# The Hyena transform split by even and odd times, with part of the first modulation and some spectrum rows on VectorE

## The chip, the core and the metric

The kernel runs on one core of one Trainium2 chip. The metric is the device time of one execution in microseconds (us), as the median of repeated runs. PE is the matmul engine (TensorE), PEld its weight loads, DVE VectorE, ACT ScalarE, POOL GpSimd and SP SyncE.

## The reference

One inference step of a two-layer backbone over 128 context tokens and 512 latent tokens with D_MODEL = 1024. Each layer modulates its input, projects it, runs windowed attention and a Hyena branch side by side, merges the two by gates, and then runs a feed-forward part. What the change touches is the modulation and the long convolution of the Hyena branch:

```python
mod = jax.nn.silu(cond) @ lp['w_ada'] + lp['b_ada']        # w_ada (1024, 6144); sh1, sc1 are its first 2048 columns
h = x * (1.0 + sc1) + sh1

def bidir_long_conv(u, h, bias):                            # u (1, L, 512), L = 512 latent or 128 context
    g = jnp.concatenate([h[:, 0], jnp.zeros((1, C)), h[:0:-1, 1]], axis=0)
    U = jnp.fft.rfft(u, n=2 * L, axis=1)
    G = jnp.fft.rfft(g, n=2 * L, axis=0)
    y = jnp.fft.irfft(U * G[None], n=2 * L, axis=1)[:, :L]
    return y + u * bias
```

h is the output of a small sine MLP times a decaying window; it depends on the weights alone, so its spectrum G can be made ahead of the layer.

## The kernel before

All of it is written by hand for each engine, in program order, with semaphores between the engines; nothing is scheduled. Every large matmul is done as three fp32r products of a value split into a high part and a low part (hi x hi, hi x lo, lo x hi). ACT makes the high part by a copy, DVE makes the low part by a subtraction. `split(g)` does this for a streamed weight chunk of up to 2048 columns (`raw` to `whi`, `wlo`; two slots), and SP loads the next chunk into `raw` once the low part of the chunk before has been made. `STREAM` is the order of the chunks and `GEMM` the order of the work.

**The opening** (once, until the first projection of q). PE makes the sine MLP, then the filter rows of both layers (`filter_rows`, 10 blocks a layer), the transforms of these (`g_spectrum`, five pairs a layer, `GSP_PAIRS` is their order), and the first two parts of the modulation, sh1 and sc1, as eight chunks `ada(0)` to `ada(7)` of four fp32 matmuls each with two output rows, whose results are transposed to columns (`col_mm`). DVE multiplies the filter rows with their windows, adds and subtracts them (`filter_blocks`) and makes low parts. ACT makes high parts and copies the spectra out of PSUM (`g_rows`), POOL writes them to DRAM (`g_spill`). The later modulation parts are not made on PE but on DVE, as products with whole rows of the transposed w_ada (`ada_t`, four instructions a chunk), and lie between the gates and the feed-forward tiles of layer 0. After `modulation`, ACT makes the modulated rows (`h_make`), POOL their low parts, and PE begins `opening(0, ...)`, the q projection.

**The Hyena stage** (once in each layer). A transform of length 2L over real input is taken as matmuls with cosine and sine matrices. Before this stage the input xu lies channel by token; PE transposes it by 128 tokens (`u_transposed`), DVE folds the four latent blocks into two sums and two differences (`ufold`), and PE transforms (`spectrum`): pair 0 is the context, pairs 1 and 2 the even frequencies of the latent tokens out of two folded blocks each, pairs 3 and 4 the odd ones out of all four blocks. A pair is a real and an imaginary PSUM row of 128 frequencies x 512 channels. DVE multiplies a pair with the stored spectrum (`prod`, `us`, six operations), ACT and DVE split the product into `yhi` and `ylo`, and PE transforms it back (`inverse`) onto all 512 times in `ax`. The matrices come in four chunks F0, I0, F1 and I1. Between them PE does the projection of the attention output (`attn_projected`, 24 matmuls each). Then comes gate 0, whose eight steps each wait for one low row made on DVE (`h_lo_row`, semaphore `hg_ready`), and DVE also joins the result, the bias and x0 for the next matmul (`hy_src`).

## Time and profile before

| | |
|---|---|
| median of 3 runs | 2062.82 us (2062.6 to 2062.84) |
| the profiled execution's own time | 2061.39 us |
| its span, first to last instruction | 2059.6 us |
| mean granted TensorE clock | 0.992 of full speed |
| PE busy | 2016.4 us, 98% of the span |
| DVE busy | 1142.6 us, 55% |
| ACT busy | 747.6 us, 36% |
| POOL busy | 184.0 us, 9% |
| PE's share of the chain that ended last | 90% |

PE's matmuls overlap each other in the pipeline: one of them is listed with a duration longer than the distance to the next one's start. So what a matmul costs is read as the distance between starts. The busy shares are averages over stages; how far another engine is from being the limit has to be read stage by stage.

### The profile page before, as it was taken

How to read it: one execution, taken by the hardware profiler on the slowest of the kernel's cores; microseconds unless marked ns; L12 is line 12 of the kernel's file. 1: busy time of each engine (PE TensorE's matmuls, PEld its weight loads, DVE VectorE, ACT ScalarE, POOL GpSimd, SP SyncE). 2: the span in 40 equal slices, each digit the busy share in tenths (PEclk: the TensorE clock that was granted, in tenths of full speed). 3: DMA queues.
4: the chain of work that ended last, by engine and by line, in shares of the span. 5: the costliest groups of instructions: out<-in, count | busy, mean ns of one | idle time of the engine just before them, and what ended most of it. 6: DMA issues, size and time to landing. Idle time of an engine off the chain costs nothing.

```text
span 2059.6 us, 30339 instructions
## 1 busy us (share of the span) xinstructions
PE 2016.4 (98%) x13030; PEld 1917.8 (93%) x13030; DVE 1142.6 (55%) x1682; ACT 747.6 (36%) x1103; POOL 184.0 (9%) x202
## 2 busy tenths in 40 slices
PE   8999999999999999999999999999999999999997
PEld 3589998999989999999998999899998999999996
DVE  6416457777556767776545454863246433233435
ACT  3354453522264321333244443452226332133323
POOL 0120001200141000000031000120015000000011
PEclk9999999999999999999999998999999999999998
DMA  8331112254313335434322101222221212212121
GB/s 313 143 124 64 39 62 92 88 179 165 125 59 123 138 133 197 178 126 154 105 71 82 65 21 60 98 77 82 82 83 47 90 63 71 90 65 79 63 71 52
DMA packets 37726, 207.07 MB, mean 101 GB/s; under 512 B 4326, under 2 KB 7959, under 8 KB 18904
## 3 DMA queue, kind: packets, MB, share of 16 engines
q1 hardware_dynamic: 31192, 185.04, 25.1%
q0 software_dynamic: 3312, 13.35, 1.8%
q10 hardware_dynamic: 3088, 6.75, 0.9%
q8 instruction: 102, 1.67, 0.3%
q14 instruction: 32, 0.26, 0.0%
HBM read 196.98 MB, written 8.14 MB: 100 GB/s over the span
## 4 chain that ended last, share of the span: by engine, by line
PE 90%; DVE 4%; ACT 3%; issue 1%; DMA 1%; SPq 0%; POOL 0%; ACTq 0%; DVEq 0%
PE gemm_psum L609 50%; PE gemm_psum L639 15%; PE gemm_psum L662 3%; PE gemm_psum L682 3%; PE gemm_psum L622 3%; PE aux_psum L749 3%; PE aux_psum L802 2%; PE gemm_psum L788 2%; PE aux_psum L730 2%; PE gemm_psum L551 2%; PE gemm_psum L515 1%; PE aux_psum L738 1%; ACT h_src_rows L1174 1%; PE aux_psum L772 1%; DMA ada_early<-in_ada 1%
## 5 line engine op out<-in xcount | busy, mean ns | idle before, releaser
L609 PE MATMUL gemm_psum<-h_hi,w_hi 128*128 128x322 f32 x2144 | 497.2, 313 | 0.3
L609 PE MATMUL gemm_psum<-h_hi,w_lo 128*128 128x322 f32 x2144 | 493.5, 311 | 0.0
L609 PE MATMUL gemm_psum<-h_lo,w_hi 128*128 128x322 f32 x2144 | 492.1, 311 | 0.0
L609 PEld LDWEIGHTS gemm_psum<-h_hi,w_hi 128*128 128x128 f32 x2144 | 362.5, 189 | 4.4 <-issue 3.1
L609 PEld LDWEIGHTS gemm_psum<-h_lo,w_hi 128*128 128x128 f32 x2144 | 362.7, 189 | 0.0
L609 PEld LDWEIGHTS gemm_psum<-h_hi,w_lo 128*128 128x128 f32 x2144 | 362.2, 189 | 0.0
L1574 DVE TENSOR_TENSOR w_lo<-w_raw,w_hi 128x2048 fp32r<-128x2048 f32 (+3 forms) x130 | 251.3, 1933 | 198.7 <-ACT w_hi L1104 197.7
L1104 ACT ACTIVATE w_hi<-w_raw 128x2048 fp32r<-128x2048 f32 (+3 forms) x130 | 209.6, 1612 | 170.1 <-PE gemm_psum L639 65.6
L1562 DVE CUSTOM_DVE_ANT_0 aux_psum<-w_raw,cond_by_row 128x1024 f32<-128x1024 f32 x160 | 190.9, 1256 | 6.9 <-DMA w_raw<-in_ada_t 6.4
L1707 DVE SCALAR_TENSOR_TENSOR x<-gemm_psum,mod,x 128x128 f32<-128x128 f32 (+2 forms) x144 | 55.4, 434 | 157.8 <-PE gemm_psum L639 128.0
L639 PE MATMUL gemm_psum<-act_hi,w_lo 128*128 128x322 f32 x616 | 141.9, 311 | 0.0
L639 PE MATMUL gemm_psum<-act_lo,w_hi 128*128 128x322 f32 x616 | 141.6, 311 | 0.0
L639 PE MATMUL gemm_psum<-act_hi,w_hi 128*128 128x322 f32 x616 | 141.5, 311 | 0.0
L1609 DVE SCALAR_TENSOR_TENSOR gate_acc<-gate_rows,par,gate_acc 128x642 f32<-128x642 f32 x88 | 80.2, 911 | 75.7 <-ACT gate_acc L1182 74.0
L1780 DVE TENSOR_TENSOR gate_acc<-gate_acc,gemm_psum 128x644 f32<-128x644 f32 x40 | 33.0, 826 | 144.1 <-PE gemm_psum L609 144.1
L639 PEld LDWEIGHTS gemm_psum<-act_hi,w_hi 128*128 128x128 f32 x616 | 104.3, 189 | 0.0
L639 PEld LDWEIGHTS gemm_psum<-act_hi,w_lo 128*128 128x128 f32 x616 | 104.2, 189 | 0.0
L639 PEld LDWEIGHTS gemm_psum<-act_lo,w_hi 128*128 128x128 f32 x616 | 103.9, 189 | 0.0
L1123 ACT ACTIVATE act_hi<-gate_acc 128x644 fp32r<-128x644 f32 x44 | 32.7, 742 | 154.0 <-DVE gate_acc L1780 147.6
L1181 ACT ACTIVATE gate_rows<-gemm_psum 128x644 f32<-128x644 f32 (+1 forms) x48 | 31.8, 663 | 144.8 <-PE gemm_psum L609 140.4
L662 PE MATMUL gemm_psum<-h_hi,w_hi 128*128 128x322 f32 x224 | 72.8, 325 | 11.6 <-POOL h_lo L2052 3.7
L1583 DVE TENSOR_TENSOR w_lo<-w_raw,w_hi 128x1024 fp32r<-128x1024 f32 x32 | 38.0, 1221 | 80.2 <-ACT w_hi L1119 80.2
(337 smaller groups left out, 3276.0 us busy)
## 6 DMA issues: line engine op xcount, KB each, us to landing
w_raw<-in_w_up SPq DMA_DIRECT2D x44, 1024.0 KB, 4.8
w_raw<-in_ada_t SPq DMA_DIRECT2D x40, 1024.0 KB, 4.7
w_raw<-in_w_down SPq DMA_DIRECT2D x32, 704.0 KB, 4.2
w_raw<-in_w_gate SPq DMA_DIRECT2D x16, 1024.0 KB, 4.7
w_raw<-in_w_z SPq DMA_DIRECT2D x12, 1024.0 KB, 4.7
w_raw<-in_w_out SPq DMA_DIRECT2D x8, 1024.0 KB, 4.7
g_kept<-g_rows_out POOLq DMA_DIRECT2D x10, 512.0 KB, 2.9
ada_early<-in_ada SPq DMA_DIRECT2D x4, 1024.0 KB, 20.4
```

The lines of the kernel that those rows point to most:

```text
L551: last = mm(gp[:, 2 + r % 2, :], w[s][:, cols_], v[:, pl, :], start=kb == 0 and n == 0, stop=kb == len(places) - 1 and n == 2)
L609: last = mm(gp[:, 2 * (t % 2) + hf, 0:HALF], w[:, off + P * kk:off + P * (kk + 1)], moving(kk, lo)[:, hf * HALF:(hf + 1) * HALF], start=kk ...
L622: last = mm(gp[:, 2 * (t % 2) + hf, 0:HALF], w[:, off + P * kk:off + P * (kk + 1)], moving(kk, lo)[:, half(hf)], start=kk == 0 and n == 0, ...
L639: last = mm(gp[:, 2 * (t % 2) + hf, 0:HALF], w[:, off + P * kk:off + P * (kk + 1)], moving(kk, lo)[:, half(hf)], start=kk == 0 and n == 0, ...
L662: last = mm(banks(c, p_, hf), w[:, P * (KD * c + kk):P * (KD * c + kk + 1)], (hlo if lo else hhi)[:, kk, half(hf)], start=kk == 0 and n == ...
L682: last = mm(gp[:, 2 * ((t0 + c) % 2) + hf, 0:HALF], w[:, P * (KD * c + kk):P * (KD * c + kk + 1)], moving(kk, lo)[:, hf * HALF:(hf + 1) * ...
L749: last = mm(ax[:, 2, HD * n:HD * (n + 1)], p_t(n)[:, P * kb:P * (kb + 1)], v[:, HD * (n % 2):HD * (n % 2 + 1)], start=kb == 0, stop=kb == ...
L1104: run(whi[s][:, 0:n], raw[st_ % 2][:, 0:n], ACT.Copy).then_inc(sem["w_hi"], raised("w_hi"))
L1562: V.tensor_tensor_reduce(out=ax[:, 2 * gr:2 * gr + 2, :].rearrange("p a b -> p (a b)"), in0=raw[n % 2][:, D_MODEL * (t % 2):D_MODEL * (t % ...
L1574: TT(wlo[s][:, 0:n], raw[STEP[(lane.layer, "g", g)] % 2][:, 0:n], f32(whi[s][:, 0:n]), ALU.subtract).then_inc(sem["w_split"], raised("w_sp ...
L1609: STT(acc[:, 1:ROW - 1], z[:, a:a + ROW - 2], w(tap), acc[:, 1:ROW - 1], ALU.mult, ALU.add).then_inc(sem[event if tap else "dve_order"], r ...
L1707: STT(x[:, m, a:b], gp[:, 2 * (t % 2) + h, a - HALF * h:b - HALF * h], mod[:, gate + m, gr:gr + 1], x[:, m, a:b], ALU.mult, ALU.add)\
```

## The change

The transform of the latent tokens is taken apart once more. The latent times are put in the order even, odd (`u_cols` takes every second token in the transposes, and the constants, filter features and windows are permuted alike). Pairs 3 and 4 now each transform only two blocks (one the even times, one the odd), and sums and differences of the two give the odd frequencies; that sum is a new step on ACT and DVE for the input (`odd_out`, `ureg`) and on POOL for the stored spectra (`g_combine`). Back-transforms write 256 of the 512 columns each, and DVE puts the halves together at the end, with two operations on each half. Four chunks of matrices become three (F0, F1, I0), and the order of the work around them is rewritten. Apart from that, the last two of the eight early modulation chunks go from PE to DVE (`ada_t(0, 6)`, `ada_t(0, 7)`, between the filter blocks of layer 1, with an own SBUF buffer `ada_out` for the products), and the last six spectrum rows of the opening are copied out by DVE (`g_rows_late`) and not by ACT.

```diff
-F0_BLOCKS, F1_BLOCKS = 14, 16
+F0_BLOCKS, F1_BLOCKS = 12, 10
-        + [("F", 0), ("pa", 0), ("I", 0), ("F", 1), ("I", 1)]
+        + [("F", 0), ("pa", 0), ("F", 1), ("I", 0)]
-    G_V = [(0, 1), (2, 3), (4, 5), (6, 7, 8, 9), (6, 7, 8, 9)]
+    G_V = [(0, 1), (2, 3), (4, 5), (6, 8), (7, 9)]
...
         g_spectrum(0, 4)
-        filter_rows(1, 4, 6)
+        filter_rows(1, 4, 8)
         ada(4)
+        filter_rows(1, 8, 10)
         g_spectrum(0, 1)
-        filter_rows(1, 6, 8)
+        g_spectrum(0, 2)
         ada(5)
-        g_spectrum(0, 2)
-        filter_rows(1, 8, 10)
-        ada(6)
-        ada(7)
         g_spectrum(1, 0)
...
-                    at = 512 * (2 * ((pair_ - 1) % 2) + o)
+                    at = 256 * (2 * (pair_ - 1) + o)
                     for n, (y, w) in enumerate(((yhi, whi), (yhi, wlo), (ylo, whi))):
-                        last = mm(ax[:, j, :], y[:, ys, o, P * j:P * (j + 1)], w[slot][:, at:at + 512],
+                        last = mm(out(j), y[:, ys, o, P * j:P * (j + 1)], parts(w[slot][:, at:at + 256]),
...
+            for n in (2, 3):
+                pe.wait_ge(sem["pa_out"], due("pa_out", n - 1))
+                attn_projected(n)
+            pe.wait_ge(sem["w_split"], due("w_split", gF1 + 1))
...
+            spectrum(3, U_V[3])
+            spectrum(4, U_V[4])
             pe.wait_ge(sem["w_split"], due("w_split", gI + 1))
...
+            for pair_ in range(1, PAIRS):
+                inverse(pair_, slot_of(gI), pair_ == 1, pair_ == PAIRS - 1)
...
+                if l and m == 1:
+                    dve.wait_ge(sem["cond_rows"], 1)
+                    ada_t(0, 6)
...
+                if l and n == 0:
+                    ada_t(0, 7)
+                if l and n == 1:
+                    first_modulation()
...
+        def g_rows_late(r0, r1):
+            for r in range(r0, r1):
+                dve.wait_ge(sem["gsp_mm"], 10 + r + 1)
+                V.tensor_copy(gst[:, GSP_PAIRS[r // 2], r % 2, :], gp[:, 2 + r % 2, :]).then_inc(sem["gsp_late"], 1)
...
+            for o in range(2):
+                first = ureg[:, 2 * o, :]
+                TT(ureg[:, 2 * o + 1, :], first, spec_bank(8 + o), ALU.subtract).then_inc(sem["usp_out"], raised("usp_out"))
+                dve.wait_ge(sem["usp_out"], now("usp_out"))
+                TT(first, first, spec_bank(8 + o), ALU.add).then_inc(sem["usp_out"], raised("usp_out"))
...
-                STT(xu[:, j, LAT], xu[:, j, LAT], parc("hy_bias", j), ax[:, j, :], ALU.mult, ALU.add)\
+                for a in range(2):
+                    STT(rows[:, a], rows[:, a], parc("hy_bias", j), same, ALU.mult, ALU.add)\
+                dve.wait_ge(sem["dve_order"], now("dve_order"))
+                for a, op in ((0, ALU.add), (1, ALU.subtract)):
+                    TT(rows[:, a], rows[:, a], turned, op).then_inc(sem["dve_order"], raised("dve_order"))
...
+        def g_combine(l):
+            for o in range(2):
+                G.tensor_tensor(g_first[:, o, :], gst[:, 3, o, :], gst[:, 4, o, :], ALU.add).then_inc(sem["g_halves"], 1)
+            pool.wait_ge(sem["g_halves"], 4 * l + 2)
+            for o in range(2):
+                G.tensor_tensor(gst[:, 4, o, :], gst[:, 3, o, :], gst[:, 4, o, :], ALU.subtract).then_inc(sem["g_halves"], 1)
```

Three places show how the rows of an engine move. The first is DVE in the opening, at the filter blocks of layer 1 (m = 1, then m = 2). Before, the next window products (`filter_prod`) follow at once:

```order
L1511 TENSOR_TENSOR filter_sums<-filter_prod 128x512
L1513 TENSOR_TENSOR d_block<-filter_prod 128x512
L1501 TENSOR_TENSOR filter_prod<-aux_psum,windows 128x512 x2
L1489 TENSOR_TENSOR filter_lo<-d_block,filter_hi 128x512
L1511 TENSOR_TENSOR filter_sums<-filter_prod 128x512
```

After the change four row products stand between them (`ISA mod` is the read of the accumulated sum):

```order
L1571 TENSOR_TENSOR d_block<-filter_prod 128x512
L1525 ISA ada_products,mod<-w_raw,cond_by_row 128x1024
L1525 ISA mod 128x1
L1525 ISA ada_products,mod<-w_raw,cond_by_row 128x1024
L1525 ISA mod 128x1
L1525 ISA ada_products,mod<-w_raw,cond_by_row 128x1024
L1525 ISA mod 128x1
L1525 ISA ada_products,mod<-w_raw,cond_by_row 128x1024
L1525 ISA mod 128x1
L1559 TENSOR_TENSOR filter_prod<-aux_psum,windows 128x512 x2
```

So the window products of m = 2 stand behind one chunk of the modulation, and the same happens once more before `first_modulation`.

The second place is DVE in the Hyena stage, between the products of pair 2 and the first low row of the odd pairs. Before, one odd pair took these rows, and the last of them are the low parts that PE waits for:

```order
L1842 TENSOR_TENSOR prod<-gemm_psum,g_spec 128x512
L1845 TENSOR_TENSOR u_spec<-gemm_psum,g_spec 128x512
L1847 TENSOR_TENSOR u_spec<-gemm_psum,g_spec 128x512
L1848 TENSOR_TENSOR prod<-gemm_psum,g_spec 128x512
L1852 TENSOR_TENSOR u_spec<-u_spec 128x512
L1857 TENSOR_TENSOR u_spec<-prod 128x512
L1587 TENSOR_TENSOR y_lo<-u_spec,y_hi 128x512 x2
```

After the change both odd pairs go through together: four sums and differences (L1920, L1922), a first block of six, and then a second block of six, four sums and the low parts as here:

```order
L1932 TENSOR_TENSOR prod<-u_blocks,g_spec 128x512 x2
L1932 TENSOR_TENSOR u_spec<-u_blocks,g_spec 128x512 x2
L1934 TENSOR_TENSOR u_blocks<-prod 128x512
L1935 TENSOR_TENSOR u_blocks<-u_spec 128x512
L1939 TENSOR_TENSOR u_spec<-u_blocks 128x512
L1939 TENSOR_TENSOR prod<-u_blocks 128x512
L1939 TENSOR_TENSOR u_spec<-u_blocks 128x512
L1939 TENSOR_TENSOR prod<-u_blocks 128x512
L1631 TENSOR_TENSOR y_lo<-u_spec,y_hi 128x512
L1631 TENSOR_TENSOR y_lo<-prod,y_hi 128x512
```

The first low row of pair 3 now stands behind 20 operations, and not behind six.

The third place is DVE behind the back-transform, where the result is joined. Before, a channel block took one operation between two low rows of gate 0:

```order
L1881 SCALAR_TENSOR_TENSOR xu<-xu,par,aux_psum 128x512 x2
L1587 TENSOR_TENSOR h_lo<-h_src_rows,h_hi 128x644
L1881 SCALAR_TENSOR_TENSOR xu<-xu,par,aux_psum 128x512
L1587 TENSOR_TENSOR h_lo<-h_src_rows,h_hi 128x644
L1881 SCALAR_TENSOR_TENSOR xu<-xu,par,aux_psum 128x512
L1587 TENSOR_TENSOR h_lo<-h_src_rows,h_hi 128x644
```

After the change it takes four of half the size:

```order
L1955 SCALAR_TENSOR_TENSOR xu<-xu,par,aux_psum 128x2x128 x2
L1959 TENSOR_TENSOR xu<-xu,aux_psum 128x2x128 x2
L1631 TENSOR_TENSOR h_lo<-h_src_rows,h_hi 128x644
L1955 SCALAR_TENSOR_TENSOR xu<-xu,par,aux_psum 128x2x128 x2
L1959 TENSOR_TENSOR xu<-xu,aux_psum 128x2x128 x2
```

Each low row of gate 0 thus stands behind four joining operations where it stood behind one.

## Rows read from the trace of the kernel before

**Rows 1.** The page's head and its busy times by engine.
```profile
span 2059.6 us, 30339 instructions
PE 2016.4 (98%) x13030; PEld 1917.8 (93%) x13030; DVE 1142.6 (55%) x1682; ACT 747.6 (36%) x1103; POOL 184.0 (9%) x202
```

**Rows 2.** The waits of PE over the whole run: us in total, times, longest.
```profile
PE gemm_psum L551 <- ACT g_rows_out L1056: 2.8, 2, 1.7
```

**Rows 3.** Timeline of PE in layer 0's Hyena stage: start us, us, instruction.
```profile
337.99 0.46 PE L772 MATMUL gemm_psum<-attn_lo,w_hi 128*128 128x322 f32 x2
...
338.28 0.46 PE L772 MATMUL gemm_psum<-attn_hi,w_lo 128*128 128x322 f32 x2
...
339.28 0.40 PE L802 MATMUL aux_psum<-w_hi,y_hi 128*128 128x512 f32 x1
...
339.51 0.39 PE L802 MATMUL aux_psum<-w_lo,y_hi 128*128 128x512 f32 x1
...
372.22 0.47 PE L682 MATMUL gemm_psum<-h_hi,w_hi 128*128 128x322 f32 x2
...
386.75 0.54 PE L609 MATMUL gemm_psum<-hy_hi,w_hi 128*128 128x322 f32 x2
```

**Rows 4.** Busy x count of PE, PEld, DVE, ACT, POOL from 372 to 387 us.
```profile
372.00:387.00 15.00, 14.93 (x100) 14.65 (x99) 14.64 (x18) 14.75 (x24) 10.93 (x7) 1.00 0.12 45
```

**Rows 5.** Timeline of PE in the opening; in brackets idle before and releaser.
```profile
61.35 3.60 PE L515 MATMUL gemm_psum<-w_raw,cs 128*2 128x512 f32 x8
...
111.58 0.39 PE L662 MATMUL gemm_psum<-h_hi,w_hi 128*128 128x322 f32 x1 [2.15 <-ACT g_rows_out L1056]
```

**Rows 6.** Timeline of DVE in the opening.
```profile
57.47 0.68 DVE L1513 TENSOR_TENSOR d_block<-filter_prod 128x512 f32<-128x512 f32 x1
...
90.19 0.17 DVE L1547 SCALAR_TENSOR_TENSOR mod<-gemm_psum,par 128x16 f32<-128x16 f32 x1
```

**Rows 7.** The page's group of products with a row of w_ada (busy, mean ns).
```profile
L1562 DVE CUSTOM_DVE_ANT_0 aux_psum<-w_raw,cond_by_row 128x1024 f32<-128x1024 f32 x160 | 190.9, 1256 | 6.9 <-DMA w_raw<-in_ada_t 6.4
```

**Rows 8.** Timeline of POOL, then of DVE, around 320 us.
```profile
319.81 5.67 POOL L2104 TENSOR_TENSOR v_lo<-u_blocks,v_hi 128x512 fp32r<-128x512 f32 x4
...
322.55 1.76 DVE L1852 TENSOR_TENSOR u_spec<-u_spec 128x512 f32<-128x512 f32 x1
```

**Rows 9.** Timeline of DVE in layer 0's Hyena stage.
```profile
319.97 0.68 DVE L1842 TENSOR_TENSOR prod<-aux_psum,g_spec 128x512 f32<-128x512 f32 x1
...
328.24 0.68 DVE L1842 TENSOR_TENSOR prod<-gemm_psum,g_spec 128x512 f32<-128x512 f32 x1
...
335.32 2.28 DVE L1574 TENSOR_TENSOR w_lo<-w_raw,w_hi 128x2048 fp32r<-128x2048 f32 x1
...
337.52 1.12 DVE L1868 SCALAR_TENSOR_TENSOR xu<-xu,par,aux_psum 128x128 f32<-128x128 f32 x4
...
343.54 0.68 DVE L1842 TENSOR_TENSOR prod<-gemm_psum,g_spec 128x512 f32<-128x512 f32 x1
...
348.90 0.68 DVE L1842 TENSOR_TENSOR prod<-gemm_psum,g_spec 128x512 f32<-128x512 f32 x1
...
373.34 1.39 DVE L1881 SCALAR_TENSOR_TENSOR xu<-xu,par,aux_psum 128x512 f32<-128x512 f32 x2
...
382.39 0.82 DVE L1587 TENSOR_TENSOR h_lo<-h_src_rows,h_hi 128x644 fp32r<-128x644 f32 x1
```

**Rows 10.** Granted clock in the opening, third from the end of the row.
```profile
113.00:114.00 1.00, 1.00 (x6) 1.00 (x5) 1.00 (x2) 0.97 (x3) 0.00 (x0) 0.50 1.01 410
```

**Rows 11.** Timeline of PE over the same attention tail in layers 0 and 1.
```profile
295.11 0.43 PE L749 MATMUL aux_psum<-par,p_t 128*128 128x64 f32 x2 [0.18 <-ACT p_t L1140]
...
305.96 0.55 PE L609 MATMUL gemm_psum<-h_hi,w_hi 128*128 128x322 f32 x2
...
1259.90 0.43 PE L749 MATMUL aux_psum<-par,p_t 128*128 128x64 f32 x2 [0.17 <-ACT p_t L1140]
...
1277.29 0.55 PE L609 MATMUL gemm_psum<-h_hi,w_hi 128*128 128x322 f32 x2
```

More of the change, by code:

```diff
@@ L72, in stream @@
 def stream():
-    order = [(0, "pre", 0), (0, "pre", 1)] + [(0, "ada", s) for s in range(ADA_EARLY, ADA_FIRST)]
+    order = [(0, "pre", 0), (0, "pre", 1)] + [(0, "ada", s) for s in (6, 4, 7, 5)]
     for layer in range(DEPTH):
@@ L1835, in _ @@
             split(gA)
[L1836 removed]
+            for p_ in range(3):
                 gr, gi = gsp[:, G_SLOT[p_], 0, :], gsp[:, G_SLOT[p_], 1, :]
@@ L2189, in _dft_constants @@
     k4 = np.arange(P)
+    two = [2 * np.arange(P) + b for b in range(2)]
     lat = []
@@ L2192, in _dft_constants @@
         re, im = forward(4 * k4 + add, DEC_SEQ // 2, N)
+        br, bi = back(4 * k4 + add, DEC_SEQ // 2, N)
         if add == 0:
```

291 lines of the change are left out of this document (174 added, 117 removed).

## The prediction, made before the changed kernel ran

> **What bounds the kernel now.** I began with the page's busy times: PE is busy for 2016.4 of 2059.6 us, DVE for little more than half [rows 1]. Then the list of PE's waits: it waits almost nowhere; one of the longest entries is 2.8 us in two pieces, for copies of spectrum rows in the opening [rows 2]. So work taken off PE shortens the kernel until another engine's chain reaches it. Then PE's timeline where the change acts. The distance of two starts is 0.233 us for 512 columns (339.28 to 339.51) and 0.148 us for 322 (337.99 to 338.28, two matmuls in between) [rows 3]. The busy times by stage show what the page's average hides: around gate 0 of layer 0, from 372 to 387 us, DVE is busy 14.64 of 15 us and ACT 14.75 [rows 4]. There PE has company already, and this decides the forecast.
>
> **What leaves PE.** Odd pairs: 12 matmuls of 512 less for each of two pairs, so 24 x 0.233 = 5.6 us in each `spectrum` stage, and 2 x 5.6 = 11.2 us in the opening for both layers' `g_spectrum`. Back-transforms: 96 matmuls a layer fall from 512 to 256 columns. No row shows 256; the price lies between half of the 512 (0.117) and the 322's 0.148. I take 0.119, since the 512 and the 322 lie nearly on a line through zero, and it is nearest to the half: 96 x 0.114 = 11.0 us a layer, at least 8.2. `ada(6)` and `ada(7)`: the eight passes of one chunk are one row of 3.60 us from 61.35 on [rows 5], of which some 0.1 lies over what follows; two chunks are 7.0 us. Four transposes of two columns less are 0.3. The sum off PE is 18.5 us in the opening and 16.6 in each layer, 51.7 in all.
>
> **The opening: DVE and ACT become the pace.** Layer 1's filter block m = 1 ends now at 57.47 + 0.68 = 58.1 us [rows 6], having waited for PE before; with the halved spectra I put its end at 56. Then `ada_t(0, 6)`: 4 x 1.256 = 5.0 us [rows 7]. At the same time POOL runs `g_combine(0)`, four additions of 128x512. The row on POOL's pace for that size is 5.67 us for four, and during it a DVE operation with both inputs in SBUF took 1.76 us, where the same line later took 0.69 [rows 8]: 1.07 us is what one of them pays. With three of the four products meeting POOL I add 3.2 us (bounds: 0 and, with six operations met, 6.4). DVE is at 64.3. PE has come to filter row 8 at about 60.5 and waits 4 us. From there DVE runs nearly without a pause to the modulation: three blocks of five operations at 0.60 (319.97 and the rows behind it, [rows 9]) are 9.3 with waits, two and two operations around `ada_t(0, 7)` 2.7, that chunk 5.0, the sums 0.8: the modulation is done at 82.1 against 90.3 now [rows 6], 8.2 earlier.
> From the modulation to the first projection matmul there are 21.3 us now (90.3 to 111.58, [rows 5]); in this stretch PE loses 24 matmuls (5.6 us), while ACT gets three high parts more and loses six copies to DVE. I take 5.6 as the gain and no more, because each spectrum row still waits for a copy of the one two before. That would be 13.8; for ACT's three high parts more I take 13.5 us for the whole opening. Bounds: 18.5, PE's full relief, and 8, if the meeting with POOL costs 6.4 and the copies on DVE queue behind the splits. The weight split and ACT's Silu on the row of conditions (one copy-sized 2048 operation) lie in ACT's idle time before its next high part, and cost nothing; without that cover they would cost 2 us. The transfer of that row, 1 MB, now goes out in the crowded start; nobody needs it before 56 us, so I cost it at nothing.
>
> **The Hyena stage: DVE again.** Its first product starts at 319.97 and the last low row of gate 0 at 382.39 for 0.8 [rows 9]. After the change DVE has these pieces, each from a row of its present timeline:
> pair 0, 8.3 (319.97 to 328.24, unchanged); the split of F1, 1280 columns, 1.4 (2048 take 2.2: 335.32 to 337.52); pair 1 6.4 (7.1 less a wait for ACT's split); pair 2 5.4 (343.54 to 348.90); the split of I0 2.2; the context's join 1.1; four sums and differences 2.8; twelve operations of two products 7.8; four sums 2.5; four low parts 2.8; the split of gate 0's weights 2.2; the context times x0 0.7; low rows 0 to 2 with ACT's pace 4.1. That reaches 367.7. From low row 2 to the end of low row 7 it is 10.9 us now; the joins add to it: a 512 operation takes 0.66 to 0.70 and a 128 one 0.28 (1.12 for four), so 256 columns are about 0.41 by the line between them, and a channel block costs 4 x 0.41 against 0.66, with one wait between: +0.9 each, +3.7 for four. Low row 7 ends at 319.97 + 61.5 = 381.5.
> PE in the same time: it does four `attn_projected` and the context back-transform before it needs an odd spectrum, reaches back-transform 3 at about 350 and finds its input not made: 8.7 us idle, until the first low part at 358.7. Back-transforms 3 and 4 end at 364.4, gate 0 then follows the low rows, and after the last one 18 matmuls remain (2.7 us): 384.2 against 386.6, where gate 0 ends now (386.75 is the next row, [rows 3]). So of 16.6 us taken off PE in a layer, 2.4 reach the end, and the rest becomes two idle stretches. Bounds: 6, if the joins cost half and no operation meets POOL, and a loss of 1, if a strided operation of 256 costs as much as one of 512. After gate 0 nothing waits longer: DVE is done 1.6 us sooner than now.
> The Trainium skill (GPSIMD Engine Reference, Specifications) says that GpSimd's SBUF interfaces are shared with VectorE and are contended by VectorE instructions with two SBUF inputs. The trace agrees in 1.76 against 0.69 us. By that rule the new products from `ureg` and the row products, both with two SBUF inputs, are exposed and the joins out of PSUM are not; it makes the time of `g_combine` worth as much as its count.
>
> **The sum.** 2061.4 (the profiled execution's own time) - 13.5 - 2 x 2.4 = 2043.1. The median of the runs stands 1.4 above the profiled one, so 2044.5.
>
> **The rivals.**
> *PE stays the only bound.* If the DVE pieces overlap better than I lay them, the 51.7 us come in full: 2011. Against it stands DVE's 14.64 of 15 us before anything is added. A half-way form, with the opening at its bound and 6 a layer, gives 2061.4 - 18.5 - 12 + 1.4 = 2032. Chance 0.12 for both.
> *The clock gives it back.* In the opening PE started again at 111.58 after a gap, and at 113 us its granted clock was 0.50, the lower level of 1.2 GHz [rows 10]. The same attention tail took 10.9 us in layer 0 (295.11 to 305.96) and 17.4 in layer 1 (1259.90 to 1277.29), where the clock was at the lower level for most of it [rows 11]: 6.5 us for one spell. Now there will be a gap of 8.7 us in each layer. If the clock is low only for back-transforms 3 and 4, they take up to 5 us more, of which 3.3 are hidden, since DVE asks for them at 367.7 only. If it stays low through gate 0 as well, its 96 matmuls at 0.268 (0.148 x 1.8) take 25.7 us and end at 395: 8.7 us later than now in each layer, in all 2061.4 + 17.4 - 13.5 + 1.4 = 2067, slower than before. It decides from about 5 us of loss a layer on. Against it: gate 0 keeps PE nearly nine tenths busy even at DVE's pace. Chance 0.05.
> The Trainium skill (TensorE: Matmul & The Clock Gate, Part 1) has it that the array idles at 1.2 GHz and sustained activity releases 2.4 GHz. By that alone the restart behind the gap is slow and then recovers within the back-transforms; the sum would be the same as mine, and only a stage with short gaps would fall to the rival.
> *The spells move.* The spell of 6.5 us in layer 1 has no cause in the program that layer 0 lacks. With another timing it may vanish (2038) or strike both layers (2051). I leave the likeliest at one and put both into the range.
> *Nothing gained.* If the meeting with POOL and the copies behind splits cost their worst (opening +8 only) and the joins cost full size, 2061.4 - 8 + 2 + 1.4 = 2057, with a second spell 2063. Chance 0.09.
>
> **How the numbers follow.** The forecast with the moving spells holds 0.74; it spans 2036 to 2054. The range for 8 in 10 takes in the half-way form and the worst bound: 2033 to 2057. About 0.2%, 4 us, is what a measurement of this kernel can tell from no change. Below 2058.7 lie the forecast, the first rival and a third of the last: 0.89; the rest of the last is within 0.2%: 0.06; above 2066.9 lies the clock's rival: 0.05.
>
> **What would show it.** PE busy about 50 us less; PE idle before back-transform 3 for 7 to 10 us in each layer, released by DVE's `y_lo`; idle steps in gate 0 released by `h_lo` on DVE; 256-column matmuls 0.12 us apart; a PE wait of 3 to 5 us for `filter_prod` near 60 us with POOL's additions beside `ada_products`; the first projection at 98 us and gate 0's end 16 us earlier than now. I am wrong if `y_lo` of pair 3 comes within 3 us of PE, if the 256-column joins measure 0.3 or 0.6, or if the clock is at 0.50 through gate 0.

## The result and the profile after

| | before | after |
|---|---|---|
| median | 2062.71 us (2061.13 to 2062.84, 4 runs) | 2029.58 us (2029.05 to 2031.81, 4 runs) |
| ratio | | 0.9843, 95% interval 0.9826 to 0.986 |
| first projection starts | 111.58 [rows 5] | 97.39 |
| PE busy | 2016.4 [rows 1] | 1963.9 |

The kernel is 33.1 us faster; 18.3 were forecast (2061.4 less 2043.1). A second occasion, told below, gave the changed kernel nearly the same time (2030.42) and the kernel before a median of 2055.89. One execution of a variant (`copies_act`), the one that was profiled, took 3191 us at a mean granted clock of 0.556; its time is left out, and of its trace only durations on DVE and POOL are used.

The page's head and its busy times by engine, after:

```profile
span 2026.9 us, 30168 instructions
...
PE 1963.9 (97%) x12914; PEld 1881.4 (93%) x12914; DVE 1168.8 (58%) x1743; ACT 740.6 (37%) x1098; POOL 195.6 (10%) x210
```

The waits of PE over the whole run (total, times, longest), after:

```profile
PE aux_psum L819 <- DVE y_lo L1631: 16.1, 2, 8.1
...
PE aux_psum L545 <- DVE filter_prod L1559: 4.6, 1, 4.6
...
PE gemm_psum L691 <- DVE h_lo L1631: 2.4, 6, 0.8
```

The timeline of PE, after, with the idle time before and its releaser in brackets:

```profile
64.57 2.93 PE L545 MATMUL aux_psum<-w,h2T 128*128 128x512 f32 x3 [4.57 <-DVE filter_prod L1559]
...
97.39 0.39 PE L671 MATMUL gemm_psum<-h_hi,w_hi 128*128 128x322 f32 x1 [0.89 <-DVE w_lo L1627]
...
297.16 0.62 PE L797 MATMUL aux_psum<-v_first,w_hi 128*128 128x512 f32 x2
...
328.29 0.28 PE L819 MATMUL aux_psum<-w_hi,y_hi 128*128 128x256 f32 x1
...
328.41 0.28 PE L819 MATMUL aux_psum<-w_lo,y_hi 128*128 128x256 f32 x1
...
342.13 0.58 PE L819 MATMUL aux_psum<-w_hi,y_hi 128*128 128x256 f32 x1 [8.03 <-DVE y_lo L1631]
...
366.58 0.46 PE L618 MATMUL gemm_psum<-hy_hi,w_hi 128*128 128x322 f32 x2
...
1256.91 0.62 PE L797 MATMUL aux_psum<-v_first,w_hi 128*128 128x512 f32 x2
...
1326.35 0.46 PE L618 MATMUL gemm_psum<-hy_hi,w_hi 128*128 128x322 f32 x2
```

PE has 116 matmuls less (48 in the two `g_spectrum`, 48 in the two `spectrum` stages, 16 of `ada`, 4 transposes) and is busy 52.5 us less, against the 51.7 of the working; both busy times hold some work at the low clock. The wait for `y_lo` is new, 8.0 us in each layer before back-transform 3 (342.13), and so is the one for `filter_prod` (64.57). 256 columns are 0.12 us apart (328.29 to 328.41).

The timeline of DVE, after:

```profile
55.94 2.29 DVE L1525 CUSTOM_DVE_ANT_0 ada_products<-w_raw,cond_by_row 128x1024 f32<-128x1024 f32 x1
...
63.83 1.28 DVE L1559 TENSOR_TENSOR filter_prod<-aux_psum,windows 128x512 f32<-128x512 f32 x2
...
82.22 0.17 DVE L1547 SCALAR_TENSOR_TENSOR mod<-mod,par 128x8 f32<-128x8 f32 x1
...
303.93 0.68 DVE L1887 TENSOR_TENSOR prod<-aux_psum,g_spec 128x512 f32<-128x512 f32 x1
...
349.98 0.83 DVE L1631 TENSOR_TENSOR h_lo<-h_src_rows,h_hi 128x644 fp32r<-128x644 f32 x1 [0.88 <-ACT h_hi L1356]
...
350.73 0.87 DVE L1955 SCALAR_TENSOR_TENSOR xu<-xu,par,aux_psum 128x256 f32<-128x256 f32 x2
...
351.63 0.75 DVE L1959 TENSOR_TENSOR xu<-xu,aux_psum 128x256 f32<-128x256 f32 x2
...
362.92 0.81 DVE L1631 TENSOR_TENSOR h_lo<-h_src_rows,h_hi 128x644 fp32r<-128x644 f32 x1
```

The modulation is done at 82.4 us (82.22 and the row's 0.17), the first product of the Hyena stage starts at 303.93 and the last low row of gate 0 ends at 363.7.

Windows of the changed kernel; the third number from the end is the granted clock. The first two and the last are its low stretches, the third is layer 1's attention tail:

```profile
62.00:69.00 7.00, 4.43 (x7) 2.23 (x8) 6.93 (x13) 0.63 (x1) 0.96 (x2) 0.51 0.85 303
...
338.00:346.00 8.00, 3.87 (x20) 3.87 (x21) 7.97 (x11) 4.19 (x7) 0.17 (x3) 0.57 0.00 0
...
1242.00:1256.00 14.00, 14.00 (x114) 14.00 (x113) 8.09 (x13) 6.00 (x11) 0.54 (x1) 1.00 0.32 115
...
1297.00:1308.00 11.00, 6.14 (x29) 6.14 (x30) 10.28 (x15) 6.43 (x11) 0.83 (x4) 0.53 0.10 23
```

And the same tail in the kernel before, [rows 11]:

```profile
1263.00:1277.00 14.00, 14.00 (x71) 14.00 (x71) 3.84 (x7) 3.20 (x6) 0.54 (x1) 0.51 0.30 109
```

**Where the time came from.** The matmuls between two marks are the same in both kernels outside the opening and the stage, so the span can be cut at marks on PE. The marks of before that [rows 3, 5] don't show are the first transform of each layer and the end of layer 1's gate 0:

```profile
313.19 0.63 PE L788 MATMUL aux_psum<-v_first,w_hi 128*128 128x512 f32 x2
...
1284.52 0.62 PE L788 MATMUL aux_psum<-v_first,w_hi 128*128 128x512 f32 x2
...
1358.07 0.54 PE L609 MATMUL gemm_psum<-hy_hi,w_hi 128*128 128x322 f32 x2
```

| stretch | before | after | gained | forecast |
|---|---|---|---|---|
| start to first projection | 111.58 | 97.39 | 14.2 | 13.5 |
| to layer 0's first transform | 201.61 | 199.77 | 1.8 | 0 |
| layer 0's first transform to the end of gate 0 | 73.56 | 69.42 | 4.1 | 2.4 |
| to layer 1's first transform | 897.77 | 890.33 | 7.4 | 0 |
| layer 1's stage, the same marks | 73.55 | 69.44 | 4.1 | 2.4 |
| to the end of the span | 701.53 | 700.55 | 1.0 | 0 |
| sum | 2059.6 | 2026.9 | 32.7 | 18.3 |

Two stretches where the change touches nothing gave 9.2 us. Both held a stretch of low clock before ([rows 10, 11]) and hold none now. They are not alike. The 7.4 us are a low stretch that is gone. The 1.8 us belong to one that can also fall earlier: in three other profiles of the kernel before (experiment 2) PE's clock is low at about 88 to 95 us (in one of them behind the first projection as well), the first projection starts at 113.1 to 113.4 and the first transform at 313.4, 313.4 and 314.7, no sooner than the 313.19 here. In the second profile of the changed kernel the clock is low from 84 to 92 us, and the first projection starts at 99.05. So the opening is uncertain by about 1.7 us in either kernel, and the first two rows are better read together: 16.0 us from these two profiles, 14.6 from the others (313.4 less 298.79), 13.5 forecast. The last stretch, 1.0 us, is within what it varies by itself (700.4 to 702.2 us in the changed kernel and its variants).

### The profile page after: what moved, and what is told of

It reads as the page before. It is cut to its first block, busy times and chain, and to the rows that moved or that the text cites. A ratio compares the mean times of both kernels' runs of the same rounds, so it can differ in the third digit from the quotient of the medians.

```text
span 2026.9 us, 30168 instructions
## 1 busy us (share of the span) xinstructions
PE 1963.9 (97%) x12914; PEld 1881.4 (93%) x12914; DVE 1168.8 (58%) x1743; ACT 740.6 (37%) x1098; POOL 195.6 (10%) x210
## 4 chain that ended last, share of the span: by engine, by line
PE 83%; DVE 10%; ACT 4%; issue 2%; ACTq 0%; DMA 0%; POOL 0%; SPq 0%; DVEq 0%
PE gemm_psum L618 51%; PE gemm_psum L648 15%; PE gemm_psum L671 3%; PE gemm_psum L631 3%; PE aux_psum L758 2%; PE gemm_psum L691 2%; PE aux_psum L739 2%; PE aux_psum L747 1%; ACT h_src_rows L1186 1%; PE gemm_psum L525 1%; DVE aux_psum L1793 1%; PE gemm_psum L563 1%; DVE w_lo L1618 1%; DVE x L1797 1%; PE aux_psum L545 1%
## 5 line engine op out<-in xcount | busy, mean ns | idle before, releaser
L1618 DVE TENSOR_TENSOR w_lo<-w_raw,w_hi 128x2048 fp32r<-128x2048 f32 (+4 forms) x128 | 244.6, 1911 | 182.1 <-ACT w_hi L1116 181.1
L1116 ACT ACTIVATE w_hi<-w_raw 128x2048 fp32r<-128x2048 f32 (+4 forms) x128 | 204.1, 1594 | 170.7 <-PE gemm_psum L648 65.6
L1135 ACT ACTIVATE act_hi<-gate_acc 128x644 fp32r<-128x644 f32 x44 | 32.7, 742 | 153.5 <-DVE gate_acc L1824 147.1
L2159 POOL TENSOR_TENSOR sums<-x 128x644 f32<-128x644 f32 x4 | 6.4, 1589 | 790.5 <-DVE x L1751 790.5
```

The source lines that it names most:

```text
L1116: run(whi[s][:, 0:n], raw[st_ % 2][:, 0:n], ACT.Copy).then_inc(sem["w_hi"], raised("w_hi"))
L1618: TT(wlo[s][:, 0:n], raw[STEP[(lane.layer, "g", g)] % 2][:, 0:n], f32(whi[s][:, 0:n]), ALU.subtract).then_inc(sem["w_split"], raised("w_sp ...
```

## The experiments

Times are medians; where a run is one execution it says so. The kernel before was measured beside each set, but since its own time turns out to fall into two groups, variants are compared with the changed kernel's 2029.6 and 2030.4, and by marks in their traces.

**1. The changed kernel again.** No edit.

> The changed kernel as it is, measured beside the kernel before on another occasion. Theory (part of the 33 us was a stretch of lower clock that the kernel before happened to have in its four executions): where the kernel before takes 2053.7 and not 2062.7, the changed kernel still takes 2029 to 2031, and the gain is 23 to 25 us, ratio 0.988. Rival (the change itself removed the stretch): the gain is 33 us, ratio 0.984.

2030.42 us (2030.23 to 2030.69, 4 runs); before 2055.89 (2053.21 to 2062.57, 9 runs); ratio 0.9871, interval 0.9851 to 0.9891. The first theory holds: the changed kernel's time stayed, and the gain fell to 25.5 us. Over all sets the kernel before ran 37 times: 16 executions at 2052.9 to 2056.8 us, 21 at 2059.6 to 2063.2, none between. Where the clock was listed the first group had a mean of 0.995 to 0.997, the second 0.991 to 0.994. Four of the sets, each on another chip, hold executions of both groups, so it is not the chip that decides. The changed kernel's eight executions lie between 2029.0 and 2031.8 (median 2030.3). Against the medians of the groups, 2053.9 and 2061.5, the gain is 24 us over the first and 31 over the second; the first occasion, with four executions of the second group, gave 33.

**2. Shifting layer 1.** The same matmul repeated in layer 0's feed-forward, 14, 28 or 56 times in the kernel before, 28 times in the changed one:

```diff
+            if lane.layer == 0 and GEMM[g] == ("down", 3):
+                for _ in range(14):
+                    mm(gp[:, 2 * (t % 2), 0:HALF], whi[s][:, off:off + P], moving(0, False)[:, half(0)], start=True, stop=True)
```

> The kernel before with 14 repeated 322-column matmuls (2.1 us) in layer 0's feed-forward, in front of a down projection; the same product is written again. It shifts all of layer 1. Theory (timing): whether the clock falls in layer 1's attention tail depends on when the tail comes, not on what the program does there: with some of the shifts of 2.1, 4.1 and 8.3 us the low stretch is shorter, longer or gone, and the time differs from 2062.7 plus the shift by up to 6.6 us. Rival (the program's own activity): the low stretch stays at the same place of the program and as long in all three, and this kernel takes 2064.8.

> The same with 28 matmuls, 4.1 us. Theory (timing): the low stretch in layer 1's attention tail (13.6 us from 1263) moves against the program, and the time is not 2062.7 + 4.1 = 2066.8. Rival (the program's own activity): 2066.8, with the stretch moved along by 4.1.

> The same with 56 matmuls, 8.3 us. Theory (timing): the low stretch in layer 1's attention tail moves against the program or is gone; gone it would be 2062.7 + 8.3 - 6.6 = 2064.4. Rival (the program's own activity): 2071.0.

> The changed kernel with the same 28 matmuls in layer 0's feed-forward, 4.1 us. Theory (timing): layer 1's attention tail, which had the full clock, may fall to the lower one: 2029.6 + 4.1 = 2033.7, or up to 6.6 more, 2040. Rival (the change itself took away what made the clock fall): the tail keeps the full clock, 2033.7.

One execution each: 2055.8, 2059.2, 2064.15 and, changed, 2034.51. The tail of the kernel before with 14 more matmuls; then the end of gate 0, the longer of the two waits of PE in the tail, and layer 1's first transform:

```profile
1263.00:1277.00 14.00, 12.81 (x107) 12.81 (x108) 8.85 (x16) 6.32 (x12) 0.54 (x1) 1.00 0.43 151
```

```profile
387.00 0.54 PE L609 MATMUL gemm_psum<-hy_hi,w_hi 128*128 128x322 f32 x2
...
1264.19 0.43 PE L752 MATMUL aux_psum<-par,p_t 128*128 128x64 f32 x2 [1.23 <-DVE p_t L1676]
...
1279.85 0.62 PE L791 MATMUL aux_psum<-v_first,w_hi 128*128 128x512 f32 x2
```

The tail has the full clock in all four. From 387.00 to 1279.85 it is 892.85 us; less the 2.1 put in, 890.8, against 897.77 before: the low stretch costs 7.0 us (by the kernels with 28 and 56 matmuls 7.0 and 6.8). That the stretch belongs to the program's own activity is refuted. That the shift removed it is not shown: the kernel before, unshifted, took 2055.62 on that occasion, in the first group too. Nor do PE's waits in the tail settle it. The kernel before waits there for 0.17 us [rows 11] and, with its clock about to fall, for 1.22:

```profile
1262.34 0.44 PE L749 MATMUL aux_psum<-par,p_t 128*128 128x64 f32 x2 [1.22 <-DVE p_t L1673]
```

The three shifted kernels wait for 0.16 to 0.18 and 1.22 to 1.23 us at the same places and keep the full clock.

**3. The two parts moved to DVE, taken back singly.** `ada_back` has `ada(6)` and `ada(7)` on PE, `rows_back` has all spectrum rows on ACT:

```diff
-ADA_ROWS = 6
+ADA_ROWS = 8
...
+        ada(6)
+        ada(7)
         g_spectrum(1, 0)
```

```diff
-    LATE_ROWS = 14
+    LATE_ROWS = 20
...
-                    if d in (1, 2):
+                    if d:
                         g_rows(1, 1 + d, 2 + d)
...
-                g_rows_late(4, 8)
```

> The changed kernel with the last two early modulation chunks back on PE (7.0 us of PE more, 10 us of DVE less); all else stays. Theory (trade): in the changed kernel PE waited 4.6 us near 60 us for DVE and then ran some 2.7 us slower at the lower clock, so the 7.0 us were given back on the spot: the wait near 60 us vanishes, the first projection stays within 1 us of 97.4 us, and the time within 2 us of the changed kernel's 2029.6. Rival (relief, as the prediction had it): the 7.0 us off PE came through to a good part: the first projection is 3 to 6 us later, at 100 to 103 us, the time about 2034.

> The changed kernel with the last six spectrum rows of the opening copied by ACT again, between its own pieces of the modulated rows. Theory (ACT's pace): a pair of ACT's modulated row and copy takes 1.9 us, a spectrum row on PE 1.4, so six rows take some 3 us more: the first projection at 100 to 101 us, the time 3 us above the changed kernel's 2029.6. Rival: DVE's copies also stand in front of the low part of the first weights, which released the first projection, so that taking them off it gives the time back: the first projection within 0.7 us of 97.4.

2033.16 (4 runs) and 2035.7 us (4 runs). PE in `ada_back`: its window matmuls start at 60.02 without a wait, but the first projection at 101.40.

```profile
60.02 1.98 PE L545 MATMUL aux_psum<-w,h2T 128*128 128x512 f32 x4
...
101.40 0.39 PE L673 MATMUL gemm_psum<-h_hi,w_hi 128*128 128x322 f32 x1 [1.04 <-DVE w_lo L1622]
```

The first projection of the changed kernel was at 97.39 in one profile and at 99.05 in that of the second occasion.

So the move of the two chunks gained 2.4 to 4.0 us there and 2.7 to 3.6 in the time: nearer to the relief than to the trade that I put first. In `rows_back` an ACT copy is what the first projection waits for:

```profile
101.10 0.61 PE L671 MATMUL gemm_psum<-h_hi,w_hi 128*128 128x322 f32 x1 [0.89 <-ACT g_rows_out L1068]
```

The first projection comes 2.1 to 3.7 us later, near the 3 expected, and the time is 5.3 to 6.1 us more. In the profiled execution, which took 2037.81 us and was the slowest of the four, another 2.5 us lie in the restart behind the first projection: it is 202.25 us to the first transform against 199.77, with the clock at 0.52 from 100 to 107 us. Whether the other three have it is not known.

**4. POOL's additions left out.** `g_combine` for layer 0 is not done, so its odd spectra stay unsplit sums.

```diff
+            if l:
                 for o in range(2):
                     G.tensor_tensor(g_first[:, o, :], gst[:, 3, o, :], gst[:, 4, o, :], ALU.add)...
```

> The changed kernel without POOL's four additions of g_combine for layer 0 (left out: layer 0's odd spectra stay the sums over even and over odd times). Theory (the additions on POOL cost DVE about 1 us for each two-input operation beside them): the row products of the first modulation chunk take 1.22 us each and not 2.2, the window products come 4 us sooner and PE's wait near 60 us is under 1 us. Rival (the products are slow there for another reason, the transfers of the opening): they take 2.2 us all the same.

One execution, 2026.88. DVE's row product, then PE's window matmuls and the first projection:

```profile
56.52 1.22 DVE L1525 CUSTOM_DVE_ANT_0 ada_products<-w_raw,cond_by_row 128x1024 f32<-128x1024 f32 x1
...
60.95 1.98 PE L545 MATMUL aux_psum<-w,h2T 128*128 128x512 f32 x4 [0.55 <-DVE filter_prod L1559]
...
94.90 0.39 PE L671 MATMUL gemm_psum<-h_hi,w_hi 128*128 128x322 f32 x1 [1.40 <-DVE w_lo L1627]
```

The product takes 1.22 us where it took 2.29 beside POOL (55.94 in the changed kernel), and PE waits 0.55 and not 4.57. By this one execution those four additions cost the kernel 3.5 us (2030.4 less 2026.9), 4.15 at the first projection (99.05 less 94.90).

**5. The first chunk later, in three steps.** `ada_later` puts `ada_t(0, 6)` behind block m = 2; `ada_later2` also puts ACT's copies first; `ada_later3` also changes the order in which SP loads.

```diff
-                if l and m == 1:
+                if l and m == 2:
                     ada_t(0, 6)
```

```diff
-        filter_hi(1, 2, 5)
-        g_rows(0, 6, 8)
+        filter_hi(1, 2, 4)
+        g_rows(0, 6, 9)
+        filter_hi(1, 4, 5)
+        g_rows(0, 9, 10)
         filter_hi(1, 5, 6)
-        g_rows(0, 8, 10)
+        first_row(2)
         filter_hi(1, 6, 7)
-        first_row(2)
```

```diff
-    order = [... for s in (6, 4, 7, 5)]
+    order = [... for s in (4, 6, 5, 7)]
```

> The changed kernel with the first modulation chunk on DVE one filter block later, behind the block m = 2. Theory (PE's wait of 4.6 us near 60 us and the 2.7 us at the lower clock behind it set the modulation): PE finds its window products done, comes 4 to 6 us sooner to the transposes, the modulation ends when DVE is through with its second chunk at about 80.5 (it is 82.3 now), and the first projection comes 1 to 2 us sooner, 95.5 to 96.5. Rival (DVE is the pace anyway): the same work in another order, the first projection at 97.4.

> As ada_later, and ACT copies the spectrum rows 6 to 9 ahead of the high parts that wait for DVE. Theory (in ada_later PE's wait only moved, to 5.8 us for a copy that stood behind a high part in ACT's queue): PE's wait near 64 us is under 1 us, the modulation is done at about 80.3 when DVE is through with its second chunk (82.2 in the changed kernel), the first projection 2 us sooner than in the changed kernel, and the time about 2028.4 against 2030.4. Rival (the end of the opening is set by ACT's pace behind the modulation): the first projection within 0.7 us of the changed kernel's.

> As ada_later2, and SP loads the early modulation chunks in the order 4, 6, 5, 7 and not 6, 4, 7, 5. Theory (in ada_later2 PE waited 7.9 us for the transfer of chunk 5, which stood in SP's queue behind that of chunk 7, and that one waited for DVE to be done with chunk 6): the wait is under 1 us, PE is at the transposes at about 75.5 us, the modulation is done when DVE is, at 80.3, the first projection comes at 97 (99 in the changed kernel on this occasion, 97.4 in its first profile), and the time is about 2028.4. Rival (another queue holds PE up in turn): transposes at 81 again, 2030.4 or more.

2032.45, 2031.46 and 2030.05 us. The first is slower: the wait at 60 us is gone, and PE waits 5.83 us for a copy. ACT's high part, at the head of ACT's queue before it, waited for DVE until 69.44:

```profile
69.44 0.63 ACT L1059 ACTIVATE filter_hi<-d_block 128x512 fp32r<-128x512 f32 x1 [7.32 <-DVE d_block L1571]
...
70.70 0.76 PE L563 MATMUL gemm_psum<-filter_hi,w_hi 128*128 128x512 f32 x1 [5.83 <-ACT g_rows_out L1068]
```

In the second the copies are in time, and PE waits for the transfer of chunk 5:

```profile
75.42 3.36 PE L525 MATMUL gemm_psum<-w_raw,cs 128*2 128x512 f32 x4 [7.91 <-DMA w_raw<-in_ada]
```

In the third PE and DVE read:

```profile
74.36 0.91 PE L599 MATMUL gemm_psum<-ident,mod_rows_first 2*128 2x2 f32 x12
...
97.72 0.39 PE L671 MATMUL gemm_psum<-h_hi,w_hi 128*128 128x322 f32 x1 [0.98 <-DVE w_lo L1628]
...
80.73 0.17 DVE L1548 SCALAR_TENSOR_TENSOR mod<-mod,par 128x8 f32<-128x8 f32 x1
```

PE is at the transposes at 74.36 (80.85 in the changed kernel) and the modulation is done at 80.9 (82.4), near the 80.3 expected; the first projection comes at 97.72, 1.3 us sooner than on the second occasion of the changed kernel and no sooner than on its first (97.39), with PE at a low clock for most of the time from 84 to 92 us. So DVE's own length sets the end of the modulation. The 2028.4 expected did not come: the median (2029.33 to 2030.43, 4 runs) is not told from the changed kernel's.

**6. The Hyena stage.** `dve_extra` does four products twice, `pe_filler` gives PE 6.7 us more ahead of back-transform 1, `copies_act` lets ACT do the one-row copies:

```diff
+                for _ in range(1 + at):
                     for to, a, b in ((prod[:, 0, :], ur, gr), ...):
```

```diff
+                    if first and o and j == 3:
+                        for _ in range(56):
+                            mm(out(j), yhi[:, ys, o, P * j:P * (j + 1)], parts(whi[slot][:, at:at + 256]), start=True, stop=True)
```

```diff
-                    V.tensor_copy(us[0:1, 0, :], prod[0:1, 1, :])...
+                        run(us[0:1, o, :], prod[0:1, 1 - o, :], ACT.Copy).then_inc(sem["y_src"], 1)
```

> The changed kernel with the four products of the second odd pair done twice (the same values written again), 2.5 us of DVE more a layer ahead of the low part that back-transform 3 waits for. Theory (DVE's chain from its first product to the last low row of gate 0 sets the stage): the idle of PE before back-transform 3 grows from 8.1 to 10.6, gate 0 ends 2.5 us later in each layer, and the time is 5 us more, 2034.6. Rival (the 8 us gap is slack that something else leaves): 2029.6.

> The changed kernel with 56 repeated 256-column matmuls ahead of back-transform 1 in both layers (the same product written again, 56 x 0.119 = 6.7 us of PE a layer, which closes most of the 8 us idle before back-transform 3). Theory (DVE sets the end of the stage, the low clock after the gap is hidden): the stretches of lower clock at 338 and 1297 us vanish, gate 0 ends within 0.5 us of where it did, the time is within 1 us of 2029.6. Rival (the clock costs): back-transforms 3 and 4 run 1.4 and 2.7 us faster and the end of the stage comes sooner, 2026 or less. Rival (PE still counts): the 13.4 us are paid, 2043.

> The changed kernel with the four one-row copies a layer (the frequency zero and the highest one, pairs 0 and 1) done by ACT and not by DVE. Theory (the length of DVE's chain sets the stage): the copies held DVE for 1.45, 0.35, 0.45 and 0.34 us; less 0.5 us for two waits on ACT that is 2.0 us a layer, so the idle before back-transform 3 shrinks from 8.1 to about 6, gate 0 ends 2 us sooner in each layer, and the time is 2025.6. Rival (PE or ACT sets it): the stage ends where it did, 2029.6; if the hand-over to ACT costs more than the copies, 2031.

2034.74 us: DVE's 2.5 us a layer come out in full. The wait is 10.62, and the stage, from 298.08 to 369.94, takes 71.86 us against 69.42.

```profile
345.55 0.58 PE L819 MATMUL aux_psum<-w_hi,y_hi 128*128 128x256 f32 x1 [10.62 <-DVE y_lo L1631]
...
369.94 0.48 PE L618 MATMUL gemm_psum<-hy_hi,w_hi 128*128 128x322 f32 x2
```

2030.4 us with the filler. The idle is 1.54 us, the clock stays at 1.00 where the gap was, and the stage takes 69.38 (299.16 to 368.54), in layer 1 69.42: 13.4 us of matmuls cost nothing, and the low clock in the gap had cost nothing either. In layer 0 the clock then falls inside gate 0, behind a wait of 1.74 us for `h_lo` at 356.71, and is back at full at about 361; the stage is no longer for it. In layer 1 it doesn't fall at all.

```profile
344.12 0.38 PE L822 MATMUL aux_psum<-w_hi,y_hi 128*128 128x256 f32 x1 [1.54 <-DVE y_lo L1634]
...
368.54 0.46 PE L618 MATMUL gemm_psum<-hy_hi,w_hi 128*128 128x322 f32 x2
...
340.00:348.00 8.00, 6.46 (x56) 6.26 (x55) 7.97 (x12) 4.20 (x7) 0.17 (x3) 1.00 0.00 0
...
358.00:360.00 2.00, 2.00 (x9) 2.00 (x9) 1.97 (x5) 1.67 (x3) 0.88 (x1) 0.50 0.00 0
```

`copies_act`: 2029.44 us, the median of the three executions at normal clock (2029.1 to 2031.14), no gain where 4 us were expected. Its only trace is that of the 3191 us execution. There the addition behind the moved copy met POOL and was held until the last of POOL's four was done:

```profile
462.27 5.06 POOL L2200 TENSOR_TENSOR v_lo<-u_blocks,v_hi 128x512 fp32r<-128x512 f32 x4
...
462.07 5.81 DVE L1903 TENSOR_TENSOR u_spec<-prod 128x512 f32<-128x512 f32 x1
```

In that execution POOL starts 3.5 us behind DVE's first product (458.76), in the changed kernel beside it (303.77 and 303.93), so this meeting does not explain the three others. What would, and is argued from the changed kernel's rows only: the copy at 308.32 takes 1.42 us beside POOL, whose additions end at 309.46; with the copy gone the next addition stands there and pays for the meeting in its place.

**7. Out of POOL's way.** `pool_split` starts two of POOL's four low parts where DVE begins pair 1; `ctx_early` then moves the context's back-transform ahead of the fourth attention projection.

```diff
+            v_rest(5, 7)
+            g_back(3, "g_odd_in")
+            pool.wait_ge(sem["w_split"], due("w_split", gF1 + 1))
+            v_rest(7, 9)
```

```diff
-            for n in (2, 3):
-                pe.wait_ge(sem["pa_out"], due("pa_out", n - 1))
-                attn_projected(n)
+            pe.wait_ge(sem["pa_out"], due("pa_out", 2))
+            attn_projected(2)
...
             last.then_inc(sem["cinv_mm"], raised("cinv_mm"))
+            pe.wait_ge(sem["pa_out"], due("pa_out", 3))
+            attn_projected(3)
```

> The changed kernel with POOL's four low parts of the Hyena input cut in two: two when the transform starts, and two only when DVE has split F1 and begins pair 1, so that each half runs beside DVE's products out of PSUM. Theory (POOL's two-input additions hold up DVE's two-input additions from SBUF, and DVE's chain sets the stage): the addition of pair 0 takes 0.7 and not 1.77 us and the one-row copy 0.4 and not 1.42, so gate 0 ends 1.5 to 2 us sooner in each layer, and the time is 3 to 4 us less, 2026. Rival (the collision only moves to pair 1): no gain, 2029.6.

> The changed kernel with POOL's low parts cut in two (as in pool_split) and, besides, the context's back-transform one attention projection earlier on PE, with ACT splitting I0 and DVE joining the context in the order that this gives. Theory (in pool_split DVE came 1.9 us sooner, and then waited 1.58 us for ACT's high part of pair 2, which stood behind the context's back-transform): that wait goes, gate 0 ends 1.3 us sooner than in pool_split in each layer, and the time is about 2.6 us below pool_split's 2029.75, 2027.1. Rival (PE's own order is the limit there, and the wait reappears at another of its results): 2029.75.

2029.75 and 2029.97 us. With the split, the addition takes 0.69 and the copy 0.41, but the low part of pair 2 then waits 1.58 us for ACT, which stands behind the context's back-transform. The stage takes 68.75 us (297.36 to 366.11), 0.65 less and not the 1.5 to 2 expected, and the median is not told from the changed kernel's:

```profile
306.70 0.69 DVE L1897 TENSOR_TENSOR u_spec<-u_spec 128x512 f32<-128x512 f32 x1
...
307.43 0.41 DVE L1900 COPY u_spec<-prod 1x512 f32<-1x512 f32 x1
...
323.54 1.29 DVE L1631 TENSOR_TENSOR y_lo<-u_spec,y_hi 128x512 fp32r<-128x512 f32 x2 [1.58 <-ACT y_hi L1135]
...
366.11 0.47 PE L618 MATMUL gemm_psum<-hy_hi,w_hi 128*128 128x322 f32 x2
```

With the back-transform earlier, the wait is at the next result of PE, the fourth attention projection, behind which ACT splits I0; the stage takes 69.16 us (298.80 to 367.96). That is the rival:

```profile
327.45 2.29 DVE L1618 TENSOR_TENSOR w_lo<-w_raw,w_hi 128x2048 fp32r<-128x2048 f32 x1 [1.57 <-ACT w_hi L1116]
```

**8. Together.** `best` is `ctx_early` with `ada_later2`, `best3` is `pool_split` with `ada_later3`.

> ctx_early and ada_later2 together. Theory: the gains add, 2030.4 - 0.7 - 2.6 - 2.0 = 2025. Rival: one of them is not there, 2027 to 2028.

> ada_later3 with POOL's low parts of the Hyena stage cut in two as in pool_split. Theory: the stage takes 68.8 and not 69.4 us in each layer, as there, and the opening is that of ada_later3: 2030.4 - 2.0 - 1.2 = 2027.2. Rival: as ada_later3's rival, less 1.2: 2029.2.

2032.35 us and 2025.95 us (2025.78 to 2027.74, 5 runs; ratio to before 0.9839, interval 0.982 to 0.9857). The first was expected at 2025 and is slower than the changed kernel: its trace has PE's wait for the transfer of chunk 5 as in `ada_later2`, 7.4 us long. `best3` is below every execution of the changed kernel, 4.5 us under its second median and 4.1 under `ada_later3` on the same occasion, where the theory had 1.2 for the cut. Its stages take 68.8 us each, which is that 1.2. Its first projection comes at 95.48, though its opening is that of `ada_later3` (97.72) to the letter: PE's mean clock from 84 to 98 us is 0.96 in the one profile and 0.76 in the other. So 2.2 us of the difference lie where the two kernels have the same code, most of it where the clock was low, and are not the edit's.

## Why the prediction was wrong

**Wrong step: "The spells move".** I said that a low stretch may vanish or come twice, left "the likeliest at one", and let the range end at 2033. The stretch in the attention tail [rows 11] went, 7.4 us in the table, and the one behind the opening [rows 10], 1.8: 9.2 of the 14.4 us by which the forecast was off. The stage adds 3.4, the last stretch 1.0 and the opening 0.7. The first value of that paragraph, 2038, has the right sign and the tail's stretch only. The lower end of the range combined it with no other error; it did not even reach the half-way form, which the text says it takes in and whose own sum is 2032. What the four executions of before had in common was taken for a property of the kernel; of its 33 other executions 16 lie in the faster group. Against that group the gain is 24 us, and the forecast is 5 short, most of it in the stage.

In each of the 15 profiles of the changed kernel and its variants at normal clock the tail has the full clock, and the changed kernel's eight times show one group where the kernel before has two. So the change made the fall rarer, though nothing in it touches this stage. How is open. PE waits 0.95 us for `p_t` in the changed tail, where the kernel before waits 0.17 and 1.22, but the shifted kernels of experiment 2 have the waits of before and the full clock, and no run varied the wait alone.

**Mis-sized: the Hyena stage, 2.4 forecast, 4.1 measured in each layer.** The mechanism is as put. PE idles 8.03 us (8.7 forecast) before back-transform 3, released by `y_lo`; it waits for `h_lo` in gate 0 (2.4 us in six pieces); `dve_extra` and `pe_filler` show DVE as the limit and PE's gain as idle time. DVE's chain took 59.8 us (303.93 to 363.7) and not 61.5. Half of the difference, 0.85, lies before the start of low row 2 (349.98 - 303.93 = 46.05, laid out as 46.9): 0.4 in the four low parts (2.4 us where 2.8 were laid out), 0.2 in pair 1 (6.2 for 6.4), the rest in rounding. The other half is in the low rows behind it (13.75 against 14.6): three of them took 0.9 to 1.15 us before and take 0.82 now. The joins were right: 1.57 us for a channel block (0.45 twice, 0.34 twice) against 0.66.

**Right: the opening, 13.5 forecast, 14.2 measured** (12.5 if the second profile's 99.05 is taken). `filter_prod` released PE after 4.57 us (4 forecast), DVE was at 63.83 (64.3), the modulation done at 82.4 (82.1), the first projection at 97.39 (98). The meeting with POOL cost 2.9 us in three row products (2.29, 2.16, 2.16 against 1.22), as priced at 3.2, and 1.07 in the operation before. The step missed that the wait is followed by a low clock (0.51 from 62 to 69 us). It cost little: `ada_later3`, where PE is at the transposes 6.5 us sooner, ends the modulation only 1.5 us sooner.

**Right: what leaves PE**, 116 matmuls and 52.5 us against 51.7, and the 256-column matmul, 0.12 apart against 0.119.

**The clock's rival** (2067) did not come. The clock did fall in each gap, and was back up before gate 0 needed it; in layer 1 the last back-transform matmul starts at 1310.2 and the join that waits for it at 1310.5, so it was a near thing. `pe_filler` is the closest to a test of it: there 322-column matmuls of gate 0 ran 0.27 us apart (two in 0.54, 358.47 to 359.01), the 0.268 for which the text gave no row, but for 3 to 4 us only, and the stage did not grow. **Rival "PE stays the only bound"** is refuted for the stage by `pe_filler`. That its half-way form, 2032, comes near the measured time is luck: it asks for 18.5 us in the opening and 6 a layer, and 14.2 and 4.1 were measured.

The Trainium skill (SBUF — State Buffer, Who interferes with whom) says that the pair of ports between DVE and GpSimd is an exclusive lock, that a DVE instruction with two SBUF inputs contends there with a GpSimd instruction that reads SBUF, and, of the two-port modes, that the first to issue holds the pair for its whole instruction and the other blocks. By that the price of a meeting is what is left of a POOL addition, whatever DVE's size. The trace agrees: two of POOL's additions take 2.57 us (`pool_split`, at 311.90), and the price is 1.07 for 512 columns (1.76 against 0.69), 1.07 for 1024 (2.29 against 1.22) and 5.1 where DVE was held for four in a row that took 5.06. The one-row copy, 1.42 against 0.41 with a single input, was not in the prediction's account; the same section names copies in the two-port mode as the other case.

## What to carry to other kernels

Before a forecast is made against one profile, cut out what the clock alone cost there: a stretch of low clock in a part that the change leaves alone may be gone next time, and both ends of the range must hold that. A wait that has been removed by moving work in one in-order queue is worth only the distance to the next queue's entry for the same result: here it went from DVE (4.6 us) to ACT (5.8) to SP (7.9) before the work itself was the limit. Where PE idles behind DVE, count DVE's instructions and their meetings with POOL, not PE's matmuls.

## What the runs showed of the hardware

The same kernel, unchanged, runs in two groups 3 to 10 us apart. The traces, one of the slower group and three lightly shifted ones of the faster, put 7 us of it into whether PE's clock falls in one attention tail. PE waits in that tail for 1.4 us in small pieces in all four, so the waits alone do not decide. The Trainium skill (TensorE: Matmul & The Clock Gate, Part 1) has the gate look at PE's activity in a free-running window that does not start with the kernel; the two groups fit this, and no run here shows it directly.

An operation of DVE that reads PSUM and SBUF was not slowed beside POOL (0.68 us for the products at 303.93 to 305.73 beside POOL's four additions, as elsewhere). Those with both inputs in SBUF were, by about 1.07 us each, and in both layers of `copies_act`, where they were held for all four additions of POOL, by 5.1 us.
